# Sparse attention inside a two-block transformer kernel: values as the stationary operand, gate and sum applied to the probabilities before their transposes

## The reference, cut to what matters

```
s_b = q k_b^T - slope * distance          # b: compressed, selected, window
p_b = softmax(where(valid, s_b, -1e30)) * valid
o   = gates[...,0:1] * (p_0 v_0) + gates[...,1:2] * (p_1 v_1) + gates[...,2:3] * (p_2 v_2)
out = o @ w_out
```

## Time and profile before

| what | value |
|---|---|
| median of 3 runs | 2691.07 us (2690.33 to 2693.34) |
| the profiled execution: its time, its span | 2691.1 us, 2689.3 us |
| TensorE matmul busy | 2664.1 us, 99% of the span |
| VectorE busy | 1691.0 us, 63% |
| ScalarE busy | 1345.2 us, 50% |
| GpSimd busy | 64.4 us, 2% |
| mean granted TensorE clock | 0.998 |

### The profile page before, as it was taken

The page is one execution under the profiler, slowest core; times in us unless marked ns, Lnnn a source line. Parts: engine busy times, 40 slices in busy tenths (PEclk is TensorE's granted clock), DMA queues, the critical chain, the costliest instruction groups (busy, mean ns, idle before and its releaser), DMA issues.

```text
span 2689.3 us, 34868 instructions
## 1 busy us (share of the span) xinstructions
PE 2664.1 (99%) x14276; PEld 2196.5 (82%) x14276; DVE 1691.0 (63%) x2492; ACT 1345.2 (50%) x1954; POOL 64.4 (2%) x85
## 2 busy tenths in 40 slices
PE   9999999999999999999999999999999999999998
PEld 8888778888888888888888788888888888887776
DVE  6686876566666666446545656666666664466666
ACT  6665455454444444435544545544444443355565
POOL 0000001000000000000200000000000000000002
PEclk9999999999999999999999999999999999999999
DMA  7867656666666666666655336566666666665544
GB/s 234 152 158 155 140 129 137 213 195 190 194 196 194 195 192 193 194 193 208 214 159 165 103 110 211 178 192 194 195 192 194 194 193 193 194 204 167 166 140 134
DMA packets 213506, 480.72 MB, mean 179 GB/s; under 512 B 15585, under 2 KB 16481, under 8 KB 212705
## 3 DMA queue, kind: packets, MB, share of 16 engines
q1 hardware_dynamic: 210848, 467.27, 59.7%
q0 software_dynamic: 2352, 11.17, 1.2%
q10 hardware_dynamic: 144, 0.05, 0.0%
HBM read 476.32 MB, written 2.10 MB: 178 GB/s over the span
## 4 chain that ended last, share of the span: by engine, by line
PE 90%; DVE 5%; ACT 3%; issue 1%; DMA 0%; POOL 0%; SPq 0%; ACTq 0%; POOLq 0%
PE PS L1138 20%; PE PS L1139 19%; PE PS L1144 19%; PE PS L1191 8%; PE PS L1197 8%; PE PS L1193 8%; DVE WL L2248 2%; ACT WH L1720 1%; PE PS L1570 1%; PE PS L1114 1%; DVE WORK L2415 1%; PE PS L1538 0%; PE PS L1549 0%; DMA RAW<-in_ab_w_in 0%; PE PS L1222 0%
## 5 line engine op out<-in xcount | busy, mean ns | idle before, releaser
L2248 DVE TENSOR_TENSOR WL<-RAW,WH 128x1024 fp32r<-128x1024 f32 x826 | 1010.8, 1225 | 817.9 <-ACT WH L1720 815.4
L1720 ACT ACTIVATE WH<-RAW 128x1024 fp32r<-128x1024 f32 x830 | 875.4, 1056 | 910.0 <-PE PS L1144 593.8
L1138 PE MATMUL PS<-WH,UTH 128*128 128x512 f32 x2396 | 952.3, 397 | 1.2 <-DVE UTL L2276 1.2
L1139 PE MATMUL PS<-WH,UTL 128*128 128x512 f32 x2396 | 936.1, 391 | 0.0
L1144 PE MATMUL PS<-WL,UTH 128*128 128x512 f32 x2396 | 644.2, 390 | 1.3 <-DVE WL L2248 1.3
L1138 PEld LDWEIGHTS PS<-WH,UTH 128*128 128x128 f32 x2396 | 450.8, 188 | 99.2 <-issue 4.8
L1144 PEld LDWEIGHTS PS<-WL,UTH 128*128 128x128 f32 x2396 | 449.9, 188 | 97.2 <-DVE WL L2248 2.1
L1139 PEld LDWEIGHTS PS<-WH,UTL 128*128 128x128 f32 x2396 | 451.3, 188 | 89.4
L1191 PE MATMUL PS<-WH,HTH 128*128 128x512 f32 x656 | 255.6, 390 | 0.0
L1193 PE MATMUL PS<-WH,HTL 128*128 128x512 f32 x656 | 255.2, 389 | 0.0
L1197 PE MATMUL PS<-WL,HTH 128*128 128x512 f32 x656 | 176.0, 389 | 0.0
(11 more groups left out here) (429 smaller groups left out, 2068.3 us busy)
## 6 DMA issues: line engine op xcount, KB each, us to landing
RAW<-in_ffn_w_gu SPq DMA_DIRECT2D x352, 512.0 KB, 4.5
RAW<-in_ffn_w_down SPq DMA_DIRECT2D x176, 512.0 KB, 4.6
RAW<-in_ab_w_in SPq DMA_DIRECT2D x128, 512.0 KB, 4.8
RAW<-in_nsa_w_in SPq DMA_DIRECT2D x80, 512.0 KB, 3.6
RAW<-in_w_in SPq DMA_DIRECT2D x64, 512.0 KB, 4.0
RAW<-in_ab_w_out SPq DMA_DIRECT2D x32, 512.0 KB, 4.4
RAW<-in_nsa_w_out SPq DMA_DIRECT2D x32, 512.0 KB, 4.2
RAW<-in_w_out SPq DMA_DIRECT2D x16, 512.0 KB, 4.5
```

Source lines behind the costliest of these rows:

```text
L1138: e.matmul(o, UTH[:, k + j, 128 * t:128 * t + 128], wh[:, j], start=k + j == 0, stop=False)
L1139: e.matmul(o, UTL[:, k + j, 128 * t:128 * t + 128], wh[:, j], start=False, stop=False)
L1720: e.activation(wh, raw, ACTF.Copy).then_inc(*a_hi.inc(s))
L2248: e.tensor_tensor(wl, raw, wh.bitcast(F32), ALU.subtract).then_inc(*v_lo.inc(s))
```

## The change: what it does

The matmul `pv` swaps its operands: the values of the group (keys on partitions, 128 channels) are stationary, and the transposed probabilities of all four heads (4 times 128 queries) move through as 512 columns. The result comes out with channels on partitions, so the running output is kept transposed and the step `ot` is not needed in this stage: a new step `ox` rounds it from memory into UTH and UTL, one ScalarE and one VectorE instruction of 512 columns for each (g, i). Since a query is now a column of the result, `rs` can't be applied there any more: VectorE multiplies the probabilities by it in `sx`, ahead of `pt`, which now waits for that product ("scaled"). The running sum takes one VectorE instruction for a branch instead of four.

```diff
@@ write_order
-            if st not in (1, 3):
+            if st == 2:
+                yield from need(*[("ox", k // 4, i) for i in range(2)])
+            elif st not in (1, 3):
                 yield from need(("ot", st, k - k % 2))
...
+    def turned(g, i):
+
+        yield from need(("read", 2, 4 * g), ("read", 2, 4 * g + 2), ("pv", g, i, 2))
+        yield
+        put("ox", g, i)
...
-          *[operand(2, k, *[("pv", k // 4, i, 2) for i in range(2)]) for k in range(0, 16, 2)])
+          *[turned(g, i) for g in range(4) for i in range(2)])
@@ tensor, pt
-                on.wait_ge(*(v_ns.of("mc", g, i) if br == 0 else a_ns.of("ex", g, i, br, 3)))
+                on.wait_ge(*v_ns.of("scaled", g, i, br))
@@ tensor, pv
-                for h in range(4):
-                    o = b[:, 128 * h:128 * h + 128]
-                    if br == 0:
-                        for u in (0, 64):
-                            x = e.matmul(o[u:u + 64], T[0:15, h, u:u + 64], VC[0:15, g], start=True, stop=True)
-                        continue
-                    c = (3584, 4608)[br - 1] + 128 * g
-                    for kk in range(kn):
-                        x = e.matmul(o, T[:, 4 * kk + h], ZN[:, kk, c:c + 128], start=kk == 0, stop=kk == kn - 1)
+                for kk in range(kn):
+                    n = 128 if br else 15
+                    V = ZN[:, kk, (3584, 4608)[br - 1] + 128 * g:][:, 0:128] if br else VC[0:15, g]
+                    x = e.matmul(b, V, T[0:n, 4 * kk:4 * kk + 4], start=kk == 0, stop=kk == kn - 1)
@@ scalar
+            def ox(g, i):
+                on.wait_ge(*p_mm.of(last_read[4 * g + 2]))
+                on.wait_ge(*v_ns.of("pv", g, i, 2))
+                e.activation(UTH[:, 4 * g:4 * g + 4, 128 * i:128 * i + 128], v3(ZN[:, i, 512 * g:512 * g + 512], 4),
+                             ACTF.Copy).then_inc(*a_ut.inc("ox", g, i))
@@ vector
+            def ox(g, i):
+                on.wait_ge(*a_ut.of("ox", g, i))
+                cs = slice(128 * i, 128 * i + 128)
+                e.tensor_tensor(UTL[:, 4 * g:4 * g + 4, cs], v3(ZN[:, i, 512 * g:512 * g + 512], 4),
+                                UTH[:, 4 * g:4 * g + 4, cs].bitcast(F32), ALU.subtract).then_inc(*v_ut.inc("ox", g, i))
@@ vector, sx
                 e.tensor_tensor(rs, rs, gv, ALU.mult).then_inc(*v_ns.inc("r", g, i, br))
+                on.wait_ge(*v_ns.last())
+                p3 = nsa_p(g, i, br)
+                e.tensor_tensor(p3, p3, bc(rs, p3.shape[2]), ALU.mult).then_inc(*v_ns.inc("scaled", g, i, br))
@@ vector, pv
-                on.wait_ge(*v_ns.of("r", g, i, br))
                 if br == 0:
-                    e.tensor_tensor(O, b, bc(rs, 128), ALU.mult).then_inc(*banks.empty(v_ns, "pv", g, i, br))
+                    e.tensor_copy(O, b).then_inc(*banks.empty(v_ns, "pv", g, i, br))
                     return
                 on.wait_ge(*v_ns.of("pv", g, i, br - 1))
-                for h in range(4):
-                    up = banks.empty(v_ns, "pv", g, i, br) if h == 3 else v_ns.inc("pv", g, i, br, h)
-                    e.scalar_tensor_tensor(out=O[:, h], in0=b[:, h], scalar=rs[:, h:h + 1], in1=O[:, h],
-                                           op0=ALU.mult, op1=ALU.add).then_inc(*up)
+                e.tensor_tensor(O, b, O, ALU.add).then_inc(*banks.empty(v_ns, "pv", g, i, br))
```

More of the change, by code:

```diff
@@ L1020, in build @@
         last_ot = {a[1]: a[2] + (a[1] > 2) for a in ORDER if a[0] == "ot"}
+        last_read = {a[3]: a[4] for a in ORDER if a[:3] == ("col", 2, len(NSA) - 1)}
+        last_ox = [a[1:] for a in ORDER if a[0] == "ox"][-1]
         col_end = {(a[1], a[2]): a[4] for a in ORDER if a[0] in ("col", "nar")}
@@ L1059, in room_of @@
             st = min(r for r in row_slots if s <= row_slots[r][-1] + 8)
+            if st == 2:
+                return v_ut.of("ox", *last_ox)
             return p_mm.of(row_slots[st][KTILES[st] + 33]) if st in (1, 3) else p_ut.of("ot", st, last_ot[st])
@@ L1180, in row @@
                     on.wait_ge(*v_ff.of("hl", st, k // 4))
+                elif st == 2:
+                    for i in range(2):
+                        on.wait_ge(*v_ut.of("ox", k // 4, i))
                 elif fresh:
@@ L1210, in ot @@
                         on.wait_ge(*v_og.of("o", k // 8, k % 8 // 4, t))
-                    elif st == 2:
-                        on.wait_ge(*v_ns.of("pv", k // 4, t, 2))
                     elif st == 4:
@@ L1761, in ot @@
                 on.wait_ge(*p_ut.of("ot", st, k))
-                gain = GN[:, k // 8:k // 8 + 1] if st == 0 else 1.0
                 e.activation(UTH[:, k:k + 2], v3(banks.ap("ot", st, k), 2), ACTF.Copy,
-                             scale=gain).then_inc(*a_ut.inc("ot", st, k))
+                             scale=GN[:, k // 8:k // 8 + 1]).then_inc(*a_ut.inc("ot", st, k))
+            @step
+            def ox(g, i):
[3 more added lines that the diff above has]
+                             ACTF.Copy).then_inc(*a_ut.inc("ox", g, i))
             @step
@@ L2300, in ot @@
                 b, hi, lo = v3(banks.ap("ot", st, k), 2), UTH[:, k:k + 2].bitcast(F32), UTL[:, k:k + 2]
[L2301 to L2306, removed]
+                e.scalar_tensor_tensor(out=lo, in0=b, scalar=GN[:, k // 8:k // 8 + 1], in1=hi, op0=ALU.mult,
+                                       op1=ALU.subtract).then_inc(*banks.empty(v_ut, "ot", st, k))
+            @step
+            def ox(g, i):
[3 more added lines that the diff above has]
+                                UTH[:, 4 * g:4 * g + 4, cs].bitcast(F32), ALU.subtract).then_inc(*v_ut.inc("ox", g, i))
             @step
@@ L2683, in sx @@
                 e.tensor_tensor(rs, rs, gv, ALU.mult).then_inc(*v_ns.inc("r", g, i, br))
+                on.wait_ge(*v_ns.last())
+                p3 = nsa_p(g, i, br)
+                e.tensor_tensor(p3, p3, bc(rs, p3.shape[2]), ALU.mult).then_inc(*v_ns.inc("scaled", g, i, br))
             @step
             def pv(g, i, br):
-                mx, ss, rs = nsa_st(g, i, br)
-                b = v3(banks.ap("pv", g, i, br), 4)
-                O = v3(ZN[:, i, 512 * g:512 * g + 512], 4)
+                b, O = banks.ap("pv", g, i, br), ZN[:, i, 512 * g:512 * g + 512]
                 on.wait_ge(*p_ns.of("pv", g, i, br))
-                on.wait_ge(*v_ns.of("r", g, i, br))
                 if br == 0:
-                    e.tensor_tensor(O, b, bc(rs, 128), ALU.mult).then_inc(*banks.empty(v_ns, "pv", g, i, br))
+                    e.tensor_copy(O, b).then_inc(*banks.empty(v_ns, "pv", g, i, br))
                     return
                 on.wait_ge(*v_ns.of("pv", g, i, br - 1))
-                for h in range(4):
-                    up = banks.empty(v_ns, "pv", g, i, br) if h == 3 else v_ns.inc("pv", g, i, br, h)
-                    e.scalar_tensor_tensor(out=O[:, h], in0=b[:, h], scalar=rs[:, h:h + 1], in1=O[:, h],
-                                           op0=ALU.mult, op1=ALU.add).then_inc(*up)
+                e.tensor_tensor(O, b, O, ALU.add).then_inc(*banks.empty(v_ns, "pv", g, i, br))
             @step
```

## The result

The changed kernel takes 2700.6 us (median of 6 runs, 2699.1 to 2702.5) against 2691.1: 1.0034 times the time before, 95% interval 1.0024 to 1.0045. That is slower by more than the 0.2% that a measurement can tell. The profiled execution took 2700.3 us with a span of 2698.5, 9.2 above the 2689.3 of before.

A forecast was written before the change was run, and what follows sets the result against it. TensorE bounds the kernel, but in two stretches VectorE and ScalarE together set its pace. 2691.1 + 5.8 (later waits less TensorE's gain) + 3.4 (clock) = 2700.3, say 2700 us; range 2692 to 2705.

The forecast's parts named there:

- TensorE's two long waits: At group 3's key transpose and group 2's second `pv`, waits of 0.74 and 1.45 us each grow by 3.8.
- The prices on VectorE: Each `sx` grows by 0.25, 0.72 or 1.26 us; each `pv` of branches 1 and 2 shrinks by 0.43.
- rival 3: Faster: VectorE's product is hidden and only TensorE's stream counts, 2691.1 - 6.2 = 2684.9 us; chance 0.08.
- Group 3: Last transposes wait for the new product and come 2.7 us later; bounds 2.3 to 3.0.
- TensorE's gain: In `pv` 0.8 us for branches 1 and 2, 2.0 for 15 keys; `ot` gone 3.4; together 6.2, of which 4.5 counts.
- the gain put down for group 0: 0.6 us of TensorE's gain lies in group 0, outside the stretches where it is lost.
- `ox` at no cost: The new step replaces equal ScalarE and VectorE work in `ot`: zero, or 1.3 us without cover.
- The clock: Behind two long TensorE waits the clock falls to 0.53 for 3.5 us, 1.7 lost each: +3.4; bounds nothing or twice.
- The sum: Over the attention, 3.8 + 3.8 + 2.7 - 4.5 = +5.8 us, between 4.2 and 7.0, plus 3.4 for clock falls.
- Clock stays: The chain slips but no clock fall follows: 2696.9 us, range 2695 to 2698.5; chance 0.16.
- Chain slips less: VectorE and ScalarE have more play, one 3.8 us term and its clock term fall away: 2694.8 us; chance 0.14.

The follow-up runs named there:

- Run 1: Changed kernel without VectorE's product of probabilities and `rs`, `pt` waiting for the exponentials as before: 2686.7 us, ratio 0.9983 to the kernel before.
- run 2: Kernel before plus the product, its wait and the plain sum in VectorE's `pv`; small matmuls and output transposes stay: 2705.2 us, ratio 1.0050.
- run 3: Changed kernel with steps `sx` moved behind the next tile's scores and maximum: 2685.6 us, ratio 0.9979; repeated, 2685.4 us, 0.9976.
- run 8: Changed kernel with the 15-key product over all 128 rows of other data, result wrong: 2700.2 us, a single execution.
- run 9: Changed kernel with `sx` moved behind the next scores and maximum, and the 15 compressed values filled with zeros to 128 rows: 2683.8 us, ratio 0.9969.
- run 4: Kernel before with steps `sx` moved behind the next scores and maximum, nothing else: 2688.6 us, ratio 0.9989.
- Runs 6: Changed kernel with 14 unused matmuls filling TensorE's wait at group 3's key transpose alone: 2699.2 us, ratio 1.0031.
- run 7: Changed kernel with 14 unused matmuls ahead of each of TensorE's two long waits: 2698.1 us, ratio 1.0024.

## Why the prediction was right, and where its terms were off

**TensorE's two long waits.** Right, in place, releaser and size. Group 1: 31.91 against 28.12 us, +3.79, predicted 3.8. Group 2: from 1525.47 us to 1557.38, 31.91, against 28.13 before (1518.19 to 1546.32), +3.78, predicted 3.8. The waits themselves, 3.56 and 2.53 us, are shorter than the 4.5 and 5.3 that a shift of 3.8 makes of them: TensorE lost part of it earlier. In the first chain that is 0.95 at the scores (1.17 us against 0.22), which with 2.82 at the bank makes the 3.8. In the second it is 0.91 us at the bank of the 15-key copy and some 1.6 in the low stretch behind it (3.4 us at 0.53). Run 1 shows that they come from the product, run 2 that nothing else of the change is needed for them, run 3 that its place in VectorE's order makes them.

**The prices on VectorE.** Groups by form, changed kernel, 1380 to 1650 us; count, busy, mean ns:

```profile
L2713 DVE TENSOR_TENSOR BIG<-PS,BIG 128x512 f32<-128x512 f32 x16 | 11.0, 688 | 13.8 <-PE PS L1578 13.8
...
L2710 DVE COPY BIG<-PS 128x512 f32<-128x512 f32 x8 | 5.5, 683 | 0.0
L2703 DVE TENSOR_TENSOR BIG<-BIG,ST 128x1024 f32<-128x1024 f32 x4 | 4.9, 1224 | 0.1
...
L2703 DVE TENSOR_TENSOR WORK<-WORK,ST 128x512 f32<-128x512 f32 x4 | 2.8, 691 | 0.1
```

They are within 5 ns of those taken from the earlier trace rows, 1227 and 686 ns, and the wait for `rs` is there: VectorE's timeline has the small product of inverse sum and gate at 1510.41 us and the large one at 1510.61, 0.20 behind it. L2713 follows at 1511.75, the predicted 1.14 later. The 3.55 us that rival 3 works out for a chain counts full durations for the four sums alone; with full durations for the five products too, 0.09 more each, it is an estimate of 4.0. The measured 3.79 goes with the spacing of starts.

**Group 3.** Predicted 2.7. From its second `qt` (1583.59 us before, 1591.62 after) to the last transposes of branch 2 the shift grows from 8.03 to 10.70 us: 2.7. The new waits are 0.76 and 1.20 us, predicted about 1.

**TensorE's gain.** Of the 6.2 us predicted, the 2.0 for the 15-key products were not there. Timeline of TensorE, changed kernel:

```profile
1408.22 1.07 PE L1156 MATMUL PS<-WL,UTH 128*128 128x512 f32 x4
1409.22 1.12 PE L1578 MATMUL PS<-BIG,WORK 15*128 15x512 f32 x2
1410.27 0.61 PE L1562 MATMUL PS<-MK,BIG 128*15 128x128 f32 x4
...
1503.82 1.02 PE L1578 MATMUL PS<-BIG 128*128 128x512 f32 x2
1504.68 1.04 PE L1562 MATMUL PS<-MK,BIG 128*128 128x128 f32 x8
...
1574.39 1.88 PE L1578 MATMUL PS<-BIG 128*128 128x512 f32 x4
1576.11 1.04 PE L1562 MATMUL PS<-MK,WORK 128*128 128x128 f32 x8
```

A full-height product of one column block takes 0.86 us to the next start, as the linear pace of the earlier trace rows gave. That of four records takes 1576.11 - 1574.39 = 1.72, as predicted (1.82 at 1557.38, right behind the long wait). The 15-key one takes 1.05, and the weight matmuls ahead of it 1.00 instead of 0.91, where the sixteen small records took 1.02 and 1.00: no gain. Runs 8 and 9 show why: the 0.09 ahead and 0.19 inside go with the 15 rows, 0.28 us each time, and not with the count of records as the forecast had assumed. It cost the sum 0.6: that was the gain put down for group 0, and the shift there is 0.74 us at its first `qt` and 0.75 at the start of the first chain. From the second long wait to the second `qt` of group 3 the stream got 3.0 us shorter (1557.38 to 1591.62, 34.24; before 1546.32 to 1583.59, 37.27), predicted 2.9. The swapped form as a whole gains 3.1 us (run 3 against run 4) to 4.6 (run 2 against the changed kernel), nearly all of it the transposes of `ot`.

**`ox` at no cost.** No wait of TensorE is laid to it (VectorE's part waits once, 1.4 us, for ScalarE's); its copies take 630 ns on ScalarE and 682 on VectorE.

**The clock.** Predicted were two falls of 1.7 us, measured was one of 2.7: the time between the two chains grew from 10.24 us (1507.95 to 1518.19) to 12.98 (1512.49 to 1525.47), with 6.8 us of it at 0.52. The sum was nearly right for the wrong distribution, which was luck: the first fall was prolonged, which the forecast had only as a bound, and the second long wait brought none. Runs 6 and 7 show that the fall belongs to the waits: filling both takes it away. By the medians that is worth 2.5 us, with intervals of the ratios that overlap. In run 8 each of the two waits, 3.57 and 3.56 us, brought a fall of its own, as predicted. Why in the changed kernel it comes behind one of the waits and not behind the other, and why it lasts twice as long, is not settled. The Trainium skill, "TensorE: Matmul & The Clock Gate", section "Why this matters for your kernels", warns of idle gaps between bursts, and the first wait bears it out; behind the second, 2.53 us, the clock stayed at 1.00.

**The sum.** Shift of the two timelines, start of the first chain to the last transposes: 0.75 us at 1480.58, + 3.79 + 2.74 + 3.78 - 2.22 + 1.86 = 10.70 us at 1631.24. Behind it the last pair of `ot` is gone (0.96 less, predicted 0.95), so the attention adds 9.0 us, where the prediction has 9.2: 0.7 too much loss for the clock and 0.6 too much gain for group 0 cancel, which is luck too. The 0.75 us ahead of it isn't shown to be the change's. It is there from the first weight products on (10.37 us before, 11.28 after), and among the runs here that start lies anywhere from 10.4 to 11.6. Behind the attention 0.7 is won back, and the whole span is 9.2 longer.

**The rivals.** Clock stays: run 7 is that case, 2698.1 against the 2696.9 worked out, and is not what happened. Chain slips less: refuted, both chains slipped in full. Faster: refuted here, but run 3 shows the condition it stood on. With the product behind the scores, VectorE's work is hidden as its 63% suggest, and the kernel is at 2685.5. That this is within 0.6 of the rival's 2684.9 is luck: 2.0 of the rival's gain is missing, and the two bank waits, which it didn't count, gave 2.2.

## What to carry to other kernels

An operation that is added to an engine with a third of its time free can cost nothing or all of its length, and what decided here is which instructions stand behind it in that engine's order and who waits for them; so look for stretches where two half-busy engines hand work to each other, and put new work behind the instruction that releases the other engine. Before a change is given up because it is slower, move the added operation: here one moved line turned 0.34% slower into 0.2% faster. A bank wait that grows by a few microseconds can cost TensorE's clock as well, so price it with the rows of the trace in which such a wait already occurs.

## What the runs showed of the hardware that was not expected

- The granted clock fell behind a wait of 3.56 us, and also some time behind one of 0.91 us (1543.70; low from 1546.1), but not behind one of 2.53 us, although it had fallen behind one of 2.58 in the kernel before. With the first wait filled, the same wait of 0.91 us brought no fall. It fell then behind the second long wait, now 3.60 us. In run 8 it fell behind both long waits and not behind the short one, there 1.20 us. In these cases a fall lasted 6.8 us (0.52 and 0.54) or some 3.4 us (0.50 to 0.53); what decides between them is open.
- A full-precision matmul whose stationary operand has 15 rows costs more than one with 128: 1.05 us instead of 0.86 for two records of 512 columns, and 0.09 us more for the full-height matmuls ahead of it. Zeros in the 113 other rows give that back (run 9).
